# Routed experts in blocks of 32 rows on four column tiles, down products two blocks late, experts in sorted order

## The reference

```
e_flat = expert_id.reshape(m)                  # m = tokens * 2, 32 experts
order = jnp.argsort(e_flat)
slot_sorted = pad_start[e_sorted] + jnp.arange(m) - raw_start[e_sorted]
xb = h_pad[slot_tok].reshape(n_blocks, EXPERT_BLOCK, d)
def run_block(args):
    xblk, e = args
    return (jax.nn.silu(xblk @ w_gate[e]) * (xblk @ w_up[e])) @ w_down[e]
y = jnp.einsum('nk,nkd->nd', gates, yb[slot].reshape(n, k, d))
```

## Time and profile before

| | us |
|---|---|
| median of 3 runs | 5780.04 (5775.88 to 5785.96) |
| the profiled execution | 5788.05 |
| its span, first to last instruction | 5785.7 |
| expert phase, layer 0 (from 2777 to 3540) | 763 |
| expert phase, layer 1 (from 4960 to 5701) | 741 |
| PE busy | 4182.2 (72% of the span) |
| instructions | 71070 |

### The profile page before, as it was taken

One profiled execution on the slowest core, in us unless ns is written; L12 is line 12 of the kernel. 1 busy time (PEld: TensorE's weight loads), 2 busy tenths in 40 slices (PEclk: granted clock), 3 DMA queues, 4 the chain that ended last, 5 costly groups with the idle time before them and its releaser, 6 DMA issues. The chain is left out here.

```text
span 5785.7 us, 71070 instructions
## 1 busy us (share of the span) xinstructions
PE 4182.2 (72%) x23474; PEld 2739.1 (47%) x23475; DVE 2196.7 (38%) x4254; ACT 1422.0 (25%) x3188; POOL 639.3 (11%) x1135
## 2 busy tenths in 40 slices
PE   5597599395876949574499983598199955497893
PEld 1385377284765838453133321487056644132331
DVE  0312544666556656624000002411677733200003
ACT  0210254343333424212011110210056622011111
POOL 0000000131322313300100002000300010100001
PEclk9798799697988969786799996799599977799997
DMA  9421100101010010133886697322510023799943
GB/s 336 147 86 68 62 9 9 38 1 25 10 25 10 0 34 1 46 128 109 312 339 235 228 377 282 118 89 76 193 49 10 11 98 105 274 364 397 374 165 145
DMA packets 350063, 778.83 MB, mean 135 GB/s; under 512 B 52000, under 2 KB 95284, under 8 KB 349796
## 3 DMA queue, kind: packets, MB, share of 16 engines
q1 hardware_dynamic: 297640, 624.64, 30.1%
q10 hardware_dynamic: 37696, 103.04, 4.6%
q0 software_dynamic: 14544, 48.79, 2.4%
HBM read 656.45 MB, written 122.58 MB: 135 GB/s over the span
## 5 line engine op out<-in xcount | busy, mean ns | idle before, releaser
L2306 PE MATMUL ex_bG<-ex_w,ex_xT 128*64 x880 | 424.7, 639 | 134.5 <-SPq L2227 77.3
L2306 PE MATMUL ex_bY<-ex_w,ex_aT 128*64 x880 | 392.6, 599 | 74.5 <-DVE ex_aT L2369 59.7
L2309 PE MATMUL ex_bG<-ex_w,ex_xT 128*64 128x512 f32 x880 | 424.7, 639 | 0.0
L367 PE MATMUL p_acc<-hT,p_wh 128*128 128x512 f32 (+1 forms) x1056 | 376.2, 356 | 24.6 <-DVE p_wl L379 24.6
L2309 PE MATMUL ex_bY<-ex_w,ex_aT 128*64 128x512 f32 x880 | 392.8, 600 | 0.0
L2306 PE MATMUL ex_bU<-ex_w,ex_xT 128*64 x880 | 386.6, 592 | 0.0
L2309 PE MATMUL ex_bU<-ex_w,ex_xT 128*64 128x512 f32 x880 | 386.6, 592 | 0.0
L2367 DVE TENSOR_TENSOR ex_a<-ex_sg,ex_bU 128x512 f32<-128x512 f32 x55 | 37.9, 688 | 917.9 <-PE ex_bU L2309 917.9
L367 PE MATMUL p_acc<-hT_rest,p_wh 128*128 128x512 f32 (+1 forms) x1056 | 375.7, 356 | 0.0
L367 PE MATMUL p_acc<-hT,p_wl 128*128 128x512 f32 (+1 forms) x1056 | 375.2, 355 | 0.0
L2306 PEld LDWEIGHTS ex_bG<-ex_w,ex_xT 128*64 128x64 f32 x880 | 127.9, 148 | 415.3 <-issue 415.3
(11 more groups left out here) (362 smaller groups left out, 8841.4 us busy)
## 6 DMA issues: line engine op xcount, KB each, us to landing
ex_w<-in_moe_w_gate SPq DMA_DIRECT2D x64, 2048.0 KB, 17.8
ex_w<-in_moe_w_up SPq DMA_DIRECT2D x64, 2048.0 KB, 21.2
ex_w<-in_moe_w_down SPq DMA_DIRECT2D x64, 2048.0 KB, 18.1
mods_w<-in_mod_w SPq DMA_DIRECT2D x24, 2048.0 KB, 13.0
projT_dram<-p_o ACTq DMA_DIRECT2D x44, 640.0 KB, 2.9
yb_dram<-ex_y ACTq DMA_DIRECT2D x55, 512.0 KB, 6.3
p_w<-in_od_w_in SPq DMA_DIRECT2D x12, 1024.0 KB, 5.1
n_x<-x_dram SPq DMA_DIRECT2D x20, 512.0 KB, 4.1
```

The source lines that it names most:

```text
L367: mm = nc.tensor.matmul(acc[u % 2][c][:, 0:n], a[:, u // 2, k, at], b[:, k, t0:t0 + n], start=k == 0 and x == 0, stop=k == KT - 1 and x == 2)
L2306: nc.tensor.matmul(bank[0:BR, :], stationary[:, k, 0:BR], w[:, ds(slot0 + (offset + k * n), 512)], start=k == 0, stop=k == tiles - 1)
L2309: m = nc.tensor.matmul(bank[BR:P, :], stationary[:, k, BR:P], w[:, at:at + 512], start=k == 0, stop=k == tiles - 1)
```

## The change

- Blocks have 32 rows, and a block is computed alone: each float32 product goes to four column tiles of 32 columns at once. For gate and up, the four tiles take the two halves of the gate columns and of the up columns (256 each); for down they take the four quarters of the output. A step's moving operand is 256 wide, before it was 512. Layer 0 has 97 blocks and layer 1 has 83; the loop runs in fours, so 98 and 86 are computed, 184 in all.
- The down product of block b stands after the gate and up products of block b + 2. Rows are gathered four blocks ahead into two buffers, results go through four buffers, and banks are doubled.
- The slot of a block is loaded into one of four registers a block ahead.
- Row transposes and hidden transposes are 8 matmuls each against the identity, on four column tiles, in place of 8 + 4 transposes of 128 x 128 per tile.
- The rows of h are stored with their columns permuted, so that a block is gathered as 128 pieces of 1 KB (`pieces`), one per partition, and the weights can be read as 16 KB (gate, up) and 8 KB (down) runs per partition, where each run was 2 KB (gate, up) or 4 KB (down).
- Experts are taken in the order largest, smallest, second largest, second smallest, and so on; an expert without rows still gets a block. Arrived weights are counted per block, by a loop of semaphore increments on SyncE.

With these counts the order has, in blocks, for layer 0: 11, 1, 8, 1, 7, 1, 6, 1, 5, 1, 5, 1, 4, 1, 4, 2, 4, 2, 3, 2, 3, 2, 3, 2, 3, 2, 2, 2, 2, 2, 2, 2. For layer 1: 18, 1, 6, 1, 6, 1, 6, 1, 5, 1, 3, 1, 3, 1, 3, 1, 3, 1, 3, 1, 2, 1, 2, 1, 2, 1, 2, 1, 2, 1, 1, 1.

```diff
@@ norm
-nc.vector.tensor_tensor(h[:, u, :], h0[:, u, :], mod[:, cond, 0, :], ALU.add).then_inc(h_done, 1)
+nc.vector.tensor_tensor(placed(h[:, u, :]), natural(h0[:, u, :]), natural(mod[:, cond, 0, :]), ALU.add).then_inc(h_done, 1)
@@ route_phase
-BR = 64
+BR = 32
...
-                c.did(V.tensor_tensor_scan(col(BEND), ones[:, 0:NE], col(NB), 0.0, ALU.mult, ALU.add))
-                c.did(V.tensor_tensor(col(BST), col(BEND), col(NB), ALU.subtract))
+                c.did(V.tensor_scalar(col(NB), col(NB), 1.0, None, ALU.max))
+                c.did(V.scalar_tensor_tensor(out=col(KEY), in0=count, scalar=-float(NE), in1=iota[:, 0:NE], op0=ALU.mult, op1=ALU.add))
+                tally(col(POS), cols_(col(KEY), NE, NE), rows_(col(KEY), NE, NE), ALU.is_lt, NE, NE)
+                c.did(V.tensor_scalar(col(POS), col(POS), 2.0, None, ALU.mult))
+                c.did(V.tensor_scalar(col(ORD), col(POS), -1.0, 2.0 * NE - 1.0, ALU.mult, ALU.add))
+                c.did(V.tensor_tensor(col(ORD), col(ORD), col(POS), ALU.min))
+                tally(col(BST), cols_(col(ORD), NE, NE), rows_(col(ORD), NE, NE), ALU.is_lt, NE, NE, cols_(col(NB), NE, NE))
...
@@ experts_phase, SyncE
-                        sp.wait_ge((g_done, u_done, y_done)[part], (1, 1, 2)[part] * tiles)
+                        sp.wait_ge((h_done, h_done, y_done)[part], tiles)
...
+                    if part:
+                        with sp.Fori(0, blocks):
+                            sp.sem_inc((w_hidden, w_down)[part - 1], 1)
@@ experts_phase, GpSimd
+                with pool.Fori(0, n) as i:
+                    for u in PAR:
+                        pool.wait_ge(xtr, 2 * i + u + 3)
+                        gather(2 * i + u + 4, u)
@@ experts_phase, TensorE
+                def turn_rows(p):
+                    for e in range(2):
+                        for g in range(4):
+                            at = e * P + g * BR
+                            t = nc.tensor.matmul(bX[p][g * BR:(g + 1) * BR, e * P:(e + 1) * P], x[:, p, at:at + BR], ident[:, :], start=True, stop=True)
+                    t.then_inc(xtr, 1)
...
+                def hidden(p, u, following=None):
+                    for c in range(XG):
+                        for e in range(2):
+                            for g in range(4):
+                                at = u * WCOLS + (0, UP)[g // 2] + (2 * c + e) * EH + g % 2 * HC
+                                m = nc.tensor.matmul(bH[p][g * BR:(g + 1) * BR, 0:HC], xT[:, p, e, c, :], w[:, at:at + HC],
+                                                     start=c == 0 and e == 0, stop=c == XG - 1 and e == 1)
+                        if c == 1 and following is not None:
+                            look(*following)
+                    m.then_inc(h_done, 1)
+
+                def down(p, u):
+                    for k in range(HT):
+                        for g in range(4):
+                            at = u * WCOLS + DOWN + k * D + g * XC
+                            m = nc.tensor.matmul(bY[p][g * BR:(g + 1) * BR, 0:XC], aT[:, p, k % 2, k // 2, :], w[:, at:at + XC], start=k == 0, stop=k == HT - 1)
+                    m.then_inc(y_done, 1)
+
+                def block_hidden(b, u, following):
+                    pe.wait_ge(w_hidden, b + 1)
+                    for v in range(WR):
+                        with pe.If_eq(slot[u], v):
+                            hidden(u % 2, v, following)
...
+                with pe.Fori(0, n) as i:
+                    for q in FOUR:
+                        b, u = 4 * i + q + 2, (q + 2) % 4
+                        block_hidden(b, u, (b + 1, (u + 1) % 4))
+                        pe.wait_ge(x_in[u % 2], 32 * i + (q // 2 * 16 + 48))
+                        pe.wait_ge(a_done, b)
+                        turn_rows(u % 2)
+                        turn_hidden(1 - u % 2)
+                        block_down(b - 2, q)
```

More of the change, by code:

```diff
@@ L2207, in load, with quads @@
+        pieces = rows.rearrange("t (c n) -> (t c) n", c=XG)
         def load(eng, col, most, least=0):
             return eng.value_load(table[0:1, col], min_val=least, max_val=most)
+        def quads(eng):
+            return load(eng, slice(T_QUAD, T_QUAD + 1), MQ, 1)
         with nc.Block() as block:
@@ L2235, in step @@
                         if before is not None:
-                            arrived(*before, part)
+                            arrived(*before, part, blocks)
                 for o in range(WR):
@@ L2251, in _ @@
                     step(NE - left + u, u, True, (u - 1, NE // WR + 1) if u else (WR - 1, NE // WR))
+                blocks = load(sp, slice(T_NB + NE - 1, T_NB + NE), CAP, 1)
                 for part in range(3):
-                    arrived((NE - 1) % WR, (NE - 1) // WR + 1, part)
+                    arrived((NE - 1) % WR, (NE - 1) // WR + 1, part, blocks)
+                for sem in (w_hidden, w_down):
+                    sp.sem_inc(sem, 4)
                 if fill:
@@ new lines, in _, with look @@
+                pe.wait_ge(a_blank, 1)
+                n = quads(pe)
+                slot = [pe.alloc_register(f"{tag}_slot{u}") for u in FOUR]
+                def look(b, u):
+                    pe.reg_load(slot[u], table[0:1, ds(b + T_CODE, 1)])
+                def turn_rows(p):
[4 more added lines that the diff above has]
+                    t.then_inc(xtr, 1)
@@ new lines, in block_down @@
+                def block_down(b, u):
+                    pe.wait_ge(w_down, b + 1)
+                    for v in range(WR):
+                        with pe.If_eq(slot[u], v):
+                            down(u % 2, v)
+                for b in FOUR:
+                    look(b, b)
+                for p in PAR:
+                    pe.wait_ge(x_in[p], 16)
+                    turn_rows(p)
+                pe.wait_ge(xT_done, 1)
+                block_hidden(0, 0, None)
+                pe.wait_ge(x_in[0], 32)
@@ new lines, in _ @@
+                rows_turned(2, 0)
+                product(0, 0)
+                hidden_turned(0, 0)
+                rows_turned(3, 1)
+                product(1, 1)
+                with dve.Fori(0, n) as i:
+                    for u in FOUR:
+                        b, p = 4 * i + u + 2, u % 2
+                        hidden_turned(b - 1, 1 - p)
+                        rows_turned(b + 2, p)
+                        product(b, p)
+                        result(b - 2, u, i)
+                hidden_turned(4 * n + 1, 1)
```

283 lines of the change are left out of this document (142 added, 141 removed).

## The result

The changed kernel takes 6659.01 us (median of 4 runs, 6656.87 to 6665.65) against 5783.0 for the kernel before (4 runs). The ratio is 1.1517, with a 95% interval of 1.1497 to 1.1537. Forecast were 5624 us and a range from 5530 to 5820.

A forecast was written before the change was run, and what follows sets the result against it. The expert phases were bound by traffic and TensorE in turns, neither full on average. 5788 (profiled) - 174 (experts) + 18 (routing) = 5632 us, less 8 for the runs' median: 5624 us, range 5530 to 5820.

The forecast's parts named there:

- Instruction fetch: TensorE's expert loop: fetching code ahead was taken as free, so nothing was added to a block's price.
- rival A: TensorE's loop of four is fetched anew, one stall at each of 45 returns; +211 us, about 5840; chance .16.
- p = 7.9: Price in us of one block on TensorE with a 6.2 us stall per loop return: 6.35 + 1.55.
- The far end: TensorE's loop: each of 10.5 instruction pieces waited for at 4.0 us, 42 us per four blocks.
- Straight code hides its fetches: TensorE outside loops: 18 pieces in 310 us left PE busy 98%, so fetching ahead is free.
- Stores: Result stores land in 6.3 us and have four buffers, 25 us, so their cost was taken as nothing.
- The block's price: TensorE's expert loop: 5.8 us of products and transposes plus 0.55 of register work, 6.35 us a block.
- Rival B: TensorE: only two of four column tiles run side by side; p = 10.5 or more, +620, about 6240; chance .05.
- C: Rival: row gathers late by a block, or GpSimd's queue behind loads; p = 6.95, +66, about 5690; chance .17.
- The walk: Expert phases: loads and blocks stepped in order; 663 and 682 us, together 1345, taken as 1330; -174 us.
- Routing: VectorE's chain between logits and `slots`, and after the scatters: about +9 us a layer, +18.
- The norm: The norm's last addition, 1.226 us 18 times, now with strided output: taken as 0, up to +22 us if doubled.

The follow-up runs named there:

- e1_loop2: The changed kernel with TensorE's expert loop holding two blocks in place of four; 5735.64 us, ratio 0.9912 to the kernel before.
- e8_poolstore: e1_loop2 with the stores of the results issued by GpSimd in place of ScalarE; 5658.20 us.
- e6_runs2k: e1_loop2 with gate and up weights read in runs of 2 KB in place of 16 KB, and h stored unpermuted; 5774.06 us.
- e10_pool2k: e8_poolstore with gate and up weights in runs of 2 KB in place of 16 KB, and h stored unpermuted; 5692.45 us.

## Why the prediction was wrong

**Instruction fetch, priced at nothing in the forecast: this step failed.** I had the pieces right (256 instructions, 10.5 per turn) and named the mechanism as rival A, with a chance of .16. I took a return of the loop as the only place that could stall, 6.2 us each, p = 7.9. Measured are some 12.9 us a block. The far end that I wrote down and left out of the range, each piece waited for at 4.0 us, is the one that happened: 136 pieces in 550 us, 4.0 us apart. That the 4.0, a gather's shortest landing, is also the spacing of the pieces is luck; and a turn takes 51.6 us for the 42 of that far end, as it asks for 13 pieces, not 10.5. "Straight code hides its fetches" was true and didn't carry over: there a piece lasted 17 us of work (18 in 310); in this loop it lasts 23 / 10.5 = 2.2 us (four blocks of 5.8), less than a landing, since about two thirds of what is fetched is skipped. That sum could have been made from the rows of before. A loop that doesn't stay is priced as pieces by their landing time, against the work in a turn, and it is the fetched code that counts, not the executed.

**Stores, at nothing for four buffers and 6.3 us of landing: wrong.** I looked at when they land, not at how long their issue lasts, what stands behind it on ScalarE and what it does to the loads. In e1_loop2 the nested pattern costs 71.5 us in layer 0 (723.1 to 651.6). What it cost in the changed kernel itself, under the fetch stalls, no run shows. Of the 112 us by which e1_loop2 lies above the forecast, e8_poolstore takes away 77.

**The block's price, 6.35: right in kind, 0.29 too high.** Sets stand 0.217 us apart for a forecast of 0.215; where TensorE is the bound a block takes 6.06 us. Rival B (two column tiles at a time) is refuted, and so is C: TensorE waits 12.1 us for rows in layer 0 and 11.5 in layer 1, nearly all of it in one wait each, of 11.2 and 11.0 us.

**The walk.** With both losses taken away, e8_poolstore's phases sum to 1332.2 us, for a forecast of 1330; as a change it is -168.2 for -174, since the prediction's 1504 lay between slightly wider marks. That is luck in part: blocks are cheaper than I took them, and traffic is 408 to 419 GB/s where the loads are the bound, for which I took 397. Both should have made the phases shorter than forecast, so something that the walk leaves out takes this back; what it is stays open. The prediction also has the walk's base once as 1345 and once, in its rivals, as 1350; the 5 us change nothing.

**Routing: right.** The changed kernel's wide operation, one of five of 1,024 elements, and the norm's last operation, against the earlier trace rows:

```profile
2736.37 1.49 DVE L2138 TENSOR_TENSOR rt_cmp<-rt_tb,rt_steps 128x1280 f32<-128x1280 f32 x1
...
2739.86 1.23 DVE L2138 TENSOR_TENSOR rt_cmp<-rt_c 128x1024 f32<-128x1024 f32 x1
```

```profile
L291 DVE TENSOR_TENSOR nb_h<-nb_h,nb_mod x18: 1904/1924/1942, 2654.6 to 5377.6; 128x1024 f32<-128x1024 f32 x18
```

From the wide operation to the first gather it takes 57.1 us in layer 0 and 49.4 in layer 1, where it took 47.5 and 40.4: +9.6 and +9.0, for a forecast of 9 each.

**The norm: taken as 0, bound 22.** The strided output made it 1.924 us for 1.226, 0.70 x 18 = 12.6 us at most. In e6_runs2k, where the output is unpermuted again, the operation takes 1.225:

```profile
L290 DVE TENSOR_TENSOR nb_h<-nb_h,nb_mod x18: 1224/1225/1226, 2652.2 to 4869.6; 128x1024 f32<-128x1024 f32 x18
```

**Arithmetic of the spans.** 849.2 (phases) + 18.6 (routing) = 867.8 of 878.2 us; the 10.4 left are close to the 12.6 that the norm can cost at most.

## What to carry to other kernels

Before unrolling a loop, count its code on the engine, the copies that are skipped included: here some 1,610 instructions on TensorE stayed and some 1,740 did not, and from there on the time was the number of pieces by 3.6 to 4.0 us, though the work was the same. When one bound hides another, a repair shows the next loss: look at each resource again after it. A DMA's cost is also its issue and the form of its pattern; compare its issue row, and its queue's packets per store, with those of the store it replaces.

## What the runs showed of the hardware

- TensorE's code comes in pieces of 16 KB, in a loop that doesn't stay one every 3.6 to 4.0 us on average (550 us by 136 to 153), and a turn asks for two or three more than its code fills.
- Four column tiles of 32 columns run side by side in fp32: 0.217 us for four matmuls of 256 columns in one pass, at a granted clock of 1.00.
- On ScalarE's queue a 128 KB store of 1 KB pieces in a nested pattern (4 outermost, 32 within) took 0.555 us to issue, up to 12.1 under load, had 4 small packets, and left holes in the loads, in one of which a quarter of the DMA engines' time was used. In a plain pattern it took 0.339 us, at most 0.407, had 16 small packets, and left none from 3200 to 3300 us.
- Weight runs of 16 KB in place of 2 KB raised full traffic from 393 to 412 GB/s (e10_pool2k, e8_poolstore, 3200 to 3300 us).
